# Two transformer stacks on one core: row sums with the squares stationary, a reciprocal of 128x4, and three output tiles side by side

## The chip, the cores and the metric

The kernel runs on one core of a Trainium2 chip. The metric is the device time of one execution in microseconds, taken as the median of several runs. Three runs of the kernel before gave 3040.9, 3040.95 and 3041.47 us.

## The reference

Two small stacks of two layers each run one after the other over a sequence of 512 tokens and a width of 1024. The first has sparse, windowed and dilated attention, the second a forgetting attention with a short convolution, a recurrent unit (RG-LRU), cross attention to a memory of 256 tokens, and gated feed-forward blocks. What the change touches are norms:

```python
def rmsnorm(x, g):
    x32 = x.astype(jnp.float32)
    y = x32 * lax.rsqrt(jnp.mean(x32 * x32, axis=-1, keepdims=True) + EPS)
    return y.astype(x.dtype) * g
...
    for layer in range(DEPTH):
        h = rmsnorm(x, g_mix_pre[layer])
        ...
        x = x + rmsnorm(y, g_mix_post[layer])
        h = rmsnorm(x, g_cross_pre[layer])
        m = rmsnorm(mem, g_mem[layer])
        y = memory_cross_attention(h, m, w_xq[layer], w_xkv[layer], w_xo[layer])
        x = x + rmsnorm(y, g_cross_post[layer])
        h = rmsnorm(x, g_ffn_pre[layer])
        y = swiglu(h, w_ffn_gu[layer], w_ffn_down[layer])
        x = x + rmsnorm(y, g_ffn_post[layer])
```

The first stack ends with such a norm over `x` too (`final`). So there are five places where the output of a linear, or `x` itself, is normed as a whole before anything can go on: `final` (after `dn1`), and the norms behind `xo0`, `dn2`, `xo1` and `dn3`. Four of them are followed at once by a norm ahead of a linear: `ab_in` (after `final`), `gu2` (after `xo0`), `c_u` (after `dn2`), `gu3` (after `xo1`). After the norm behind `dn3` comes the output.

## The kernel before

Activations lie feature-major: `x` is 128 partitions by 8 tiles (KT) by 512 tokens. A linear is a loop over output tiles of 128 features. Each sums 8 products (22 in the down projection) into one of the banks 0 to 3 of PSUM. The arithmetic is fp32 split in two parts, so a product is three matmuls of 128x512: `w_hi` by `xh`, `w_hi` by `xl`, `w_lo` by `xh` (lines 516 to 518).

The weights come as 462 chunks of 512 KB. They go through a ring of four slots (RING), and LEAD is 3. SyncE loads `w_raw`. ScalarE rounds it to `w_hi` (`high`, line 903, in its program order at the steps of each linear). GpSimd subtracts to get `w_lo` (`lows`, line 453). A slot is free again when TensorE is through the chunk (`chunk_done`), and an output bank when VectorE has evacuated it (`evac_done`).

A norm ahead of a linear is split. The gain goes into `xh` and `xl` before the product (`publish`), and the factor `rstd` of each token is multiplied in when the bank is evacuated (`scaled`, line 1276). `publish` for a tile m is, on ScalarE, the square into `acc` or `tmpa` (line 910) and then `xh` (line 915); on VectorE, the addition of the square to `acc` (line 1246) and then `xl` (line 1253). TensorE waits in the first output tile for each `xl` (`x_tile_ready`), and computes after that tile the sum over partitions with a matrix of ones (`sum_squares`, line 582), which leaves the sum of each token on all 128 partitions. `inverse_rms` is a scaling on VectorE (line 1264), the root on ScalarE (line 922), and the reciprocal on VectorE (line 1267), each over 128x512.

In the five places named above the same three steps stand with nothing beside them: TensorE has ended the linear, VectorE copies the last bank (line 1525, or adds it to `x`, line 1384), ScalarE squares it, VectorE adds, TensorE sums, then `inverse_rms`, and then per tile a multiplication by `rstd` (line 1529), an addition to `x` with a gain (line 1530), and `publish` of the tile before. At `final` the multiplication and the gain are one operation (line 1517).

Of the linears that follow, `gate_up` (`gu2`, `gu3`: 44 output tiles) works in pairs: tiles 2j and 2j+1 are evacuated, SiLU on ScalarE, product on VectorE, `hh` on ScalarE (line 1000), `hl` on VectorE (line 1363). ScalarE splits the weights of a pair at the head of the pair. `ab_in` has 25 tiles, of which tile 0 holds the logits of the forget gates. The sums of these (lines 1589 to 1600, a chain of small operations on 8x512) are computed on VectorE right after that tile. `c_u` has 8 tiles, each followed on VectorE by a convolution of four taps (lines 1652 and 1654) and a split (line 1660), and feeds the recurrent unit.

The order on each engine is the order of its program; engines meet at semaphores alone.

## Time and profile before

| | |
|---|---|
| median of 3 runs | 3040.95 us |
| the profiled execution | 3041.29 us, its span 3039.5 us |
| TensorE busy | 2818.8 us (93%), mean granted clock 0.961 |
| VectorE busy | 1111.0 us (37%) |
| ScalarE busy | 1089.0 us (36%) |
| GpSimd busy | 1314.0 us (43%) |
| DMA | 251.75 MB, mean 83 GB/s |

Times in the rows below are in microseconds from the start of the span unless ns is said. PE is TensorE, PEld its weight loads, DVE VectorE, ACT ScalarE, POOL GpSimd. L516 is line 516 of the kernel.

### The profile page before, as it was taken

What the parts mean: (1) busy time and instruction counts of PE and PEld (TensorE: products, weight loads), DVE (VectorE), ACT (ScalarE), POOL (GpSimd) and SP (SyncE); (2) the same over time, 40 slices, a digit from 0 to 9 for tenths busy, and PEclk for the clock granted to TensorE, in tenths of its full rate; (3) what the DMA queues carried; (4) which work ended last, traced back from release to release, by engine and by line L of the source; (5) the groups of instructions that cost most, each with busy time, mean ns of one, the idle gap of its engine ahead of it and who ended that gap; (6) DMA issues with size and microseconds to landing.
All of it is one profiled execution on the core that took longest, in us unless ns stands there. A gap on an engine that the chain in (4) does not pass through costs nothing.

```text
span 3039.5 us, 37582 instructions
## 1 busy us (share of the span) xinstructions
PE 2818.8 (93%) x13318; PEld 2219.7 (73%) x13318; DVE 1111.0 (37%) x1969; ACT 1089.0 (36%) x1761; POOL 1314.0 (43%) x691
## 2 busy tenths in 40 slices
PE   7999999999989999979998979999878789799997
PEld 5757788888657888857768857888756578588885
DVE  5674322113553222051547342221184472522202
ACT  5665322223663232232244333222225343323221
POOL 4555444444484444424446424444423364244442
PEclk9999999999999999999999989999989899799998
DMA  4301232333202223313113112233212231122331
GB/s 150 117 2 49 90 97 92 96 102 94 76 12 90 92 90 97 101 62 97 62 56 124 57 56 89 91 97 98 96 49 70 90 125 49 62 90 90 96 104 56
DMA packets 69088, 251.75 MB, mean 83 GB/s; under 512 B 7672, under 2 KB 7928, under 8 KB 68736
## 3 DMA queue, kind: packets, MB, share of 16 engines
q1 hardware_dynamic: 67104, 244.35, 25.5%
q10 hardware_dynamic: 1888, 6.14, 0.6%
q8 instruction: 59, 0.97, 0.1%
q14 instruction: 37, 0.30, 0.0%
HBM read 248.36 MB, written 2.10 MB: 82 GB/s over the span
## 4 chain that ended last, share of the span: by engine, by line
PE 83%; DVE 11%; issue 2%; ACT 2%; POOL 1%; DMA 0%; DVEq 0%; POOLq 0%; ACTq 0%
PE ps L516 25%; PE ps L517 25%; PE ps L518 25%; PE ps L611 3%; PE ps L636 2%; PE ps L622 2%; DVE acc L1246 1%; DVE xl L1253 1%; DVE rstd L1267 1%; DVE x L1530 1%; PE ps L582 1%; DVE y_mid L1529 1%; POOL pr L490 1%; DVE u_r L1654 1%; DVE u_r L1652 1%
## 5 line engine op out<-in xcount | busy, mean ns | idle before, releaser
L453 POOL TENSOR_TENSOR w_lo<-w_raw,w_hi 128x1024 fp32r<-128x1024 f32 x462 | 1117.2, 2420 | 1552.6 <-ACT w_hi L903 1547.6
L516 PE MATMUL ps<-xh,w_hi 128*128 128x512 f32 x2384 | 968.7, 406 | 88.3 <-DVE xl L1253 77.3
L517 PE MATMUL ps<-xl,w_hi 128*128 128x512 f32 x2384 | 959.2, 402 | 0.0
L518 PE MATMUL ps<-xh,w_lo 128*128 128x512 f32 x2384 | 944.6, 396 | 0.0
L903 ACT ACTIVATE w_hi<-w_raw 128x1024 fp32r<-128x1024 f32 x462 | 485.1, 1053 | 591.5 <-PE ps L518 590.7
L516 PEld LDWEIGHTS ps<-xh,w_hi 128*128 128x128 f32 x2384 | 451.7, 189 | 234.1 <-issue 72.3
L518 PEld LDWEIGHTS ps<-xh,w_lo 128*128 128x128 f32 x2384 | 453.9, 190 | 114.2
L517 PEld LDWEIGHTS ps<-xl,w_hi 128*128 128x128 f32 x2384 | 453.9, 190 | 103.5 <-issue 3.2
L516 PE MATMUL ps<-hh,w_hi 128*128 128x512 f32 x704 | 278.5, 396 | 0.0
L517 PE MATMUL ps<-hl,w_hi 128*128 128x512 f32 x704 | 278.4, 396 | 0.0
L518 PE MATMUL ps<-hh,w_lo 128*128 128x512 f32 x704 | 278.4, 395 | 0.0
L996 ACT ACTIVATE tmpa<-tmpa 128x512 f32<-128x512 f32 x88 | 55.6, 632 | 458.8 <-DVE tmpa L1276 458.8
L1276 DVE TENSOR_TENSOR tmpa<-ps,rstd 128x512 f32<-128x512 f32 x88 | 60.8, 691 | 415.2 <-PE ps L518 415.1
L490 POOL TENSOR_SCALAR pr<-pr,wgt 128x256 f32<-128x256 f32 (+3 forms) x160 | 158.1, 1001 | 94.7 <-DVE wgt L1340 94.4
L958 ACT ACTIVATE pr<-pr,negm 128x512 f32<-128x512 f32 (+2 forms) x224 | 120.1, 536 | 115.2 <-DVE negm L1326 115.1
L517 PEld LDWEIGHTS ps<-hl,w_hi 128*128 128x128 f32 x704 | 132.3, 188 | 31.9
L518 PEld LDWEIGHTS ps<-hh,w_lo 128*128 128x128 f32 x704 | 132.4, 188 | 31.9
L516 PEld LDWEIGHTS ps<-hh,w_hi 128*128 128x128 f32 x704 | 132.4, 188 | 31.9
L1276 DVE TENSOR_TENSOR tmpb<-ps,rstd 128x512 f32<-128x512 f32 x96 | 66.4, 692 | 180.6 <-PE ps L518 180.1
L1384 DVE TENSOR_TENSOR x<-ps,x 128x512 f32<-128x512 f32 x32 | 22.1, 692 | 286.2 <-PE ps L518 286.2
L1326 DVE CUSTOM_DVE_ANT_0 pr<-ps,tab 128x512 f32<-128x512 f32 (+2 forms) x192 | 85.5, 477 | 73.1 <-PE ps L611 72.0
L910 ACT ACTIVATE tmpa<-x 128x512 f32<-128x512 f32 x77 | 48.5, 630 | 165.9 <-DVE x L1384 101.0
(234 smaller groups left out, 2877.5 us busy)
## 6 DMA issues: line engine op xcount, KB each, us to landing
w_raw<-weights_in SPq DMA_DIRECT2D x462, 512.0 KB, 3.5
x<-x_in ACTq DMA_DIRECT2D x4, 512.0 KB, 10.3
mem<-mem_in ACTq DMA_DIRECT2D x2, 1024.0 KB, 4.8
x_out<-x SPq DMA_DIRECT2D x4, 512.0 KB, 2.6
rope<-rope_in ACTq DMA_DIRECT2D x1, 512.0 KB, 11.9
tab<-tables_in ACTq DMA_DIRECT2D x2, 256.0 KB, 2.9
tab<-tables_in ACTq DMA_DIRECT2D x1, 384.0 KB, 12.3
small<-small_in ACTq DMA_DIRECT2D x1, 326.5 KB, 5.0
```

The lines of the kernel that those rows point to most:

```text
L453: nc.gpsimd.tensor_tensor(w_lo[:, slot], w_raw[:, slot], w_hi.bitcast(f32)[:, slot], ALU.subtract).then_inc(lo_ready, 1)
L490: ins = nc.gpsimd.tensor_scalar(p, p, w, None, ALU.mult)
L516: nc.tensor.matmul(dst, w_hi[:, slot, w], hi, start=first, stop=False)
L517: nc.tensor.matmul(dst, w_hi[:, slot, w], lo, start=False, stop=False)
L518: return nc.tensor.matmul(dst, w_lo[:, slot, w], hi, start=False, stop=last)
L611: last = nc.tensor.matmul(ps[:, S_BANKS[n % 3], 0:u["nk"]], q, k, start=c == 0, stop=c == parts - 1)
L622: last = nc.tensor.transpose(ps[:, PT_BANKS[a], tokens(kb)], pr[:, n % 8, tokens(kb)], ident[:])
L636: last = nc.tensor.matmul(ps[rows, g["bank"], tokens(column)], values[kb], pt[:, (n + a) % 4, tokens(kb)], start=st["opens"] and kb == 0, ...
L903: A(w_hi[:, s], w_raw[:, s], ACT.Copy).then_inc(hi_ready, 1)
L958: A(p, p, ACT.Exp, scale=-1.0, bias=negm[:, slot, a:a + 1], accum_out=den[:, slot, a:a + 1]).then_inc(p_ready, 1)
L1276: return V.tensor_tensor(dst, bank[0:rows, 0:n], r[0:rows, 0:n], ALU.mult)
L1326: V.tensor_tensor_reduce(out=pr[:, n % 8, 0:nk], in0=ps[:, S_BANKS[n % 3], 0:nk], in1=u["mask"], scale=-u["scale"], scalar=start, op0=ALU.add,
```

## The change

It does five things.

1. In the five exposed norms the square of the last tile is not added to `acc`. `row_sums` takes the squares as the stationary operand and one column of ones as the moving one: four matmuls for `acc` (tiles 0 to 6), four for the last square, which leave 128x4 sums (partition = token within its block of 128). Scaling, root and reciprocal run on this 128x4 tile `stat`. `broadcast_rows` turns it back: four matmuls with a column of `stat` broadcast to 128x128 as stationary and the identity as moving operand fill bank 7 (MISC) with the reciprocal roots on all partitions. The normed tiles are computed from that bank, into banks 4 to 6, and added to `x` from there. After `xo` and `dn` ScalarE squares the last tile straight from its bank, and VectorE copies it afterwards. The table of the root is loaded ahead (`load_root`).
2. In the norms ahead of `ab_in`, `gu2`, `c_u` and `gu3` the squares are added on GpSimd (`sum_up`), six additions of 128x512, and the last is again left to the matmuls. ScalarE makes `xh` before the square (`publish_first`).
3. The first three output tiles of these four linears run side by side: for each of the 8 input tiles the products of all three (`side_by_side_tiles`). Row sums and broadcast run inside tile 3, ahead of its second and fourth input tile. The bank is then copied to `rstd` (`inverse_rms_kept`).
4. ScalarE's `high` for step 0 of these linears moves: the chunk is split ahead of the publishing, and GpSimd's order follows.
5. In `ab_in` the forget sums move from tile 0 to tile 4 on VectorE, and ScalarE's part of them from steps 0 and 1 to steps 4 and 5.

The diff, cut to its core:

```diff
+TOGETHER = {"ab_in": 3, "gu2": 3, "c_u": 3, "gu3": 3}
...
+            def sum_up(name):
+                first = list(TOGETHER).index(name) * (KT - 1)
+                before = sum(ADDS[n] for n in SUMS[:SUMS.index(name)])
+                for m in range(1, KT - 1):
+                    pool.wait_ge(sq_ready, first + m + 1)
+                    if m > 1:
+                        pool.wait_ge(acc_ready, before + m - 1)
+                    nc.gpsimd.tensor_tensor(acc[:], acc[:], tmpa[:, m % 2], ALU.add).then_inc(acc_ready, 1)
...
+            lows(CHUNK0["out_o"] + LEAD, CHUNK0["ab_in"] + LEAD + 1)
+            sum_up("ab_in")
+            lows(CHUNK0["ab_in"] + LEAD + 1, CHUNK0["ab_out"] + LEAD)
...
+                        if k in hooks:
+                            hooks[k]()
...
+                def side_by_side_tiles(n_m):
+                    pe.wait_ge(evac_done, g0 + n_m - 4)
+                    pe.wait_ge(lo_ready, c0 + n_m)
+                    for k in range(n_k):
+                        ready(k)
+                        for m in range(n_m):
+                            hi, lo = rhs(m, k)
+                            last = product(ps[:, (g0 + m) % 4, 0:n], (c0 + m) % RING, k, hi, lo,
+                                           k == 0, k == n_k - 1)
+                            if k == n_k - 1:
+                                last.then_inc(chunk_done, 1)
...
+                together = TOGETHER.get(name, 1)
+                if together > 1:
+                    side_by_side_tiles(together)
+                    for m in range(together, RING):
+                        out_tile(m, None, {1: row_sums, 3: broadcast_rows} if m == together else {})
+                    first = 1
...
+            def row_sums():
+                accs.n += KT - 2
+                rows_s.next()
+                pe.wait_ge(vt_copied, vts.n)
+                pe.wait_ge(acc_ready, accs.n)
+                for t in range(TB):
+                    nc.tensor.matmul(ps[:, MISC, t:t + 1], acc[:, tokens(t)], ones[:, 0:1], start=t == 0,
+                                     stop=False)
+                pe.wait_ge(last_sq, rows_s.n)
+                for t in range(TB):
+                    last = nc.tensor.matmul(ps[:, MISC, t:t + 1], tmpa[:, 1, tokens(t)], ones[:, 0:1],
+                                            start=False, stop=t == TB - 1)
+                last.then_inc(ss_done, 1)
+            def broadcast_rows():
+                pe.wait_ge(rows_ready, rows_s.n)
+                for t in range(TB):
+                    last = nc.tensor.matmul(ps[:, MISC, tokens(t)], stat[:, 2, t:t + 1].broadcast_to([P, P]),
+                                            ident[:], start=True, stop=True)
+                last.then_inc(rstd_ready, 1)
...
+            def square_row(src, m):
+                if m >= 3:
+                    act.wait_ge(acc_ready, n_.acc.n + m - 2)
+                if m == KT - 1:
+                    n_.acc.n += KT - 2
+                    A(tmpa[:, 1], src, ACT.Square).then_inc(last_sq, 1)
+                    return None
+                return A(acc[:] if m == 0 else tmpa[:, m % 2], src, ACT.Square)
...
+            def publish_first(m, gname):
+                A(xh[:, m], x[:, m], ACT.Copy, scale=gain(gname, m)).then_inc(xh_ready, 1)
+                ins = square_row(x[:, m], m)
+                if ins is not None:
+                    ins.then_inc(sq_ready, 1)
...
+                    if i is None and j == 0 and name in TOGETHER:
+                        root_rows()
+                    else:
+                        high(c0 + 2 * j + LEAD, i, 4)
                     high(c0 + 2 * j + 1 + LEAD, i, 4)
...
+            def squares_out(name, y, n_k=1):
+                for m in range(KT):
+                    for q in range(n_k):
+                        high(CHUNK0[name] + n_k * m + q + LEAD)
+                    if m == KT - 2:
+                        load_root()
+                    if m < KT - 1:
+                        act.wait_ge(evac_done, BANK0[name] + m + 1)
+                        square_row(y[:, m], m).then_inc(xh_ready, 1)
+                    else:
+                        act.wait_ge(chunk_done, CHUNK0[name] + n_k * KT)
+                        square_row(ps[:, (BANK0[name] + m) % 4, :], m)
+                root_rows()
...
+            def renormed_first(name, gname):
+                high(CHUNK0[name] + LEAD)
+                for m in range(KT):
+                    act.wait_ge(x_ready, n_.x.next())
+                    publish_first(m, gname)
...
+            def inverse_rms_rows(eps):
+                dve.wait_ge(ss_done, n_.ss.next())
+                V.tensor_scalar(stat[:, 1], ps[:, MISC, 0:TB], 1.0 / D, eps, ALU.mult, ALU.add).then_inc(var_done, 1)
+                dve.wait_ge(sd_done, n_.sd.next())
+                V.reciprocal(stat[:, 2], stat[:, 1]).then_inc(rows_ready, 1)
+                dve.wait_ge(rstd_ready, n_.rows.next())
+            def inverse_rms_kept(eps):
+                inverse_rms_rows(eps)
+                link(V.tensor_copy(rstd[:], ps[:, MISC, :]))
...
-            inverse_rms(rstd, 1e-5)
+            inverse_rms_rows(1e-5)
             for m in range(KT):
                 x_updated(V.scalar_tensor_tensor(out=x[:, m], in0=x[:, m], scalar=gain("final", m),
-                                                 in1=rstd[:], op0=ALU.mult, op1=ALU.mult))
+                                                 in1=ps[:, MISC, :], op0=ALU.mult, op1=ALU.mult))
                 if m:
-                    publish(m - 1, "mix_pre0")
-            publish(KT - 1, "mix_pre0")
+                    publish_first(m - 1, "mix_pre0")
+            publish_first(KT - 1, "mix_pre0")
...
+            def copies_out(name, y, n_k=1):
+                for m in range(KT):
+                    if m < KT - 1:
+                        dve.wait_ge(chunk_done, CHUNK0[name] + n_k * (m + 1))
+                    else:
+                        dve.wait_ge(last_sq, n_.rows.n + 1)
+                    V.tensor_copy(y[:, m], ps[:, (BANK0[name] + m) % 4, :]).then_inc(evac_done, 1)
+                    if m < KT - 1:
+                        publish_square(m)
+            def add_normed_rows(y, name, gname=None):
+                x0 = n_.x.n
+                def normed(m):
+                    if m >= 3:
+                        dve.wait_ge(x_ready, x0 + m - 2)
+                    return mark(V.tensor_tensor(ps[:, 4 + m % 3, :], y[:, m], ps[:, MISC, :], ALU.mult))
+                def add(m, n):
+                    dve.wait_ge(dve_self, n)
+                    x_updated(V.scalar_tensor_tensor(out=x[:, m], in0=ps[:, 4 + m % 3, :], scalar=gain(name, m),
+                                                     in1=x[:, m], op0=ALU.mult, op1=ALU.add))
+                add(0, normed(0))
+                n = normed(1)
+                for m in range(1, KT):
+                    after = normed(m + 1) if m < KT - 1 else None
+                    add(m, n)
+                    n = after
+                    if gname:
+                        publish_first(m - 1, gname)
+                if gname:
+                    publish_first(KT - 1, gname)
...
+                if m == 4:
+                    forget_sums()
+                if m == 5:
```

## Rows read from the trace of the kernel before

**Rows 1.** The page, part 4: shares of the chain that ended last.
```profile
PE 83%; DVE 11%; issue 2%; ACT 2%; POOL 1%; DMA 0%; DVEq 0%; POOLq 0%; ACTq 0%
```

**Rows 2.** Waits of TensorE: us in total, times, longest.
```profile
PE ps L516 <- DVE xl L1253: 77.3, 33, 18.4
...
PE ps L516 <- DVEq L1598: 5.5, 1, 5.5
```

**Rows 3.** Stretches around norms; each engine's busy us and instructions, clock, DMA.
```profile
core 0: us, PE busy (x) PEld busy (x) DVE busy (x) ACT busy (x) POOL busy (x), PEclk, DMA share, GB/s
1322.03:1334.10 12.07, 2.04 (x2) 0.53 (x3) 8.34 (x9) 4.72 (x7) 0.00 (x0) 0.58 0.13 43
1334.10:1347.70 13.60, 8.83 (x24) 4.71 (x25) 12.77 (x20) 8.61 (x14) 1.06 (x1) 0.87 0.00 1
1347.70:1359.60 11.90, 11.90 (x51) 9.23 (x50) 9.17 (x7) 3.50 (x4) 3.70 (x2) 1.00 0.16 45
1371.15:1376.00 4.85, 4.85 (x13) 3.85 (x14) 2.65 (x4) 3.50 (x4) 3.06 (x2) 0.58 0.03 8
...
1807.36:1826.37 19.01, 12.91 (x25) 7.19 (x26) 17.04 (x26) 8.98 (x14) 1.99 (x1) 0.50 0.00 0
...
3017.07:3039.50 22.43, 1.10 (x2) 0.30 (x2) 16.94 (x21) 2.54 (x3) 0.00 (x0) 0.58 0.23 94
```

**Rows 4.** The chain in order of time around `xo0`: start, us, what.
```profile
1795.20 0.24 PE ps L518
...
1796.19 0.64 ACT tmpa L910
...
1797.70 1.30 PE ps L582 x2
...
1800.41 3.37 DVE rstd L1267
...
1803.80 0.70 DVE y_mid L1529
...
1804.52 0.75 DVE x L1530
...
1828.07 0.43 PE ps L516
```

**Rows 5.** The same chain, small matmuls of the first attention.
```profile
145.41 1.10 PE ps L726 x8
```

**Rows 6.** Groups by line and form: count, busy us and mean ns, idle.
```profile
L1340 DVE RECIPROCAL wgt<-den 128x2 f32<-128x2 f32 x112 | 17.4, 155 | 0.5 <-ACT pr L958 0.4
...
L982 ACT ACTIVATE lp<-lp 128x8 f32<-128x8 f32 x1 | 0.2, 209 | 0.0
```

**Rows 7.** Timeline while GpSimd subtracts, stage `xkv0`.
```profile
1616.16 5.14 POOL L453 TENSOR_TENSOR w_lo<-w_raw,w_hi 128x1024 fp32r<-128x1024 f32 x2 [7.89 <-ACT w_hi L903]
...
1616.43 2.63 DVE L1529 TENSOR_TENSOR y_mid<-y_mid,rstd 128x512 f32<-128x512 f32 x1
```

**Rows 8.** Instructions of line 1253, of tile `rstd`: ns min/median/max.
```profile
L1253 DVE SCALAR_TENSOR_TENSOR xl<-x,small,xh x80: 739/745/2884, 15.6 to 2647.8; 128x512 fp32r<-128x512 f32 x80
...
L1276 DVE TENSOR_TENSOR tmpb<-ps,rstd x96: 691/692/693, 318.2 to 2888.3; 128x512 f32<-128x512 f32 x96
```

**Rows 9.** The page, part 5: the costliest groups, the two that split weights.
```profile
L453 POOL TENSOR_TENSOR w_lo<-w_raw,w_hi 128x1024 fp32r<-128x1024 f32 x462 | 1117.2, 2420 | 1552.6 <-ACT w_hi L903 1547.6
...
L903 ACT ACTIVATE w_hi<-w_raw 128x1024 fp32r<-128x1024 f32 x462 | 485.1, 1053 | 591.5 <-PE ps L518 590.7
```

**Rows 10.** Timeline of VectorE, first and last of the forget sums.
```profile
1354.39 0.47 DVE L1590 TENSOR_SCALAR fw<-fw,small 8x512 f32<-8x512 f32 x1
...
1371.04 0.07 DVE L1600 MEMSET gated<- 128x8 f32 x1
```

**Rows 11.** The chain at `dn2` and at the first evacuation of `c_u`.
```profile
2193.51 0.25 PE ps L518
...
2230.65 0.70 DVE z_u L1276
```

157 lines of the change are left out of this document (93 added, 64 removed).

## The prediction

> **What bounds the kernel now.** First the chain that ended last [rows 1]: 83% of it is TensorE, 11% VectorE. So the kernel is a stream of matmuls with holes, and the question is what fills the holes. Second the waits of TensorE [rows 2]: the largest is 77.3 us in 33 waits for `xl` of line 1253, the low half of a normed input; one wait of 5.5 us is for VectorE's line 1598, the forget sums. Third the stretches around the norms [rows 3]. A product (one matmul of 512 columns) costs 11.90 us / 51 = 0.233 us at full clock, so an output tile of 24 products takes 5.6 us. Between the last product before a norm and the first after it lie 12.07 us at `final` (1322.03 to 1334.10). Then the first tile of `ab_in` runs at the pace of the publishing: 24 products in 13.60 us, and at `gu2` 24 products in 19.01 us with VectorE busy 17.04 of them and a granted clock of 0.50, that is 1.2 GHz. Fourth the chain through one norm, `xo0` [rows 4]: TensorE ends at 1795.44 (call it t), copy, square 0.64, sum, ones matmul 1.30, variance, root, reciprocal 3.37, and only at t+8.36 the first multiplication by `rstd`.
>
> **The change, part by part.** All offsets are from t, the end of the last product before the norm.
>
> 1. *The exposed chain, five times (`final`, `xo0`, `dn2`, `xo1`, `dn3`).* Removed: the last addition, the 128x512 ones matmul, and three 128x512 operations, the reciprocal of 3.37 us [rows 4] among them. Added: 16 matmul instructions with the squares stationary (4 token blocks, two parts, two instructions each), of which 8 run under ScalarE's square; three operations on 128x4; 8 instructions that turn the reciprocal back. For the matmul instructions the nearest row is 8 of 128x64 in 1.10 us [rows 5]; the trace has none with one moving column. Bounds: 0.5 us (hardly more than a start) and 2.1 us (the same at half clock) for 8; I take 1.0. For the 128x4 operations the nearest rows are 155 ns (128x2 reciprocal) and 209 ns (128x8 on ScalarE) [rows 6]; with hand-overs of 0.03 to 0.14 us I take 0.8 us for all three, bounds 0.6 and 1.3. The sum for `xo` and `dn`: square from the bank to t+0.7; first sums to t+1.0, second to t+2.1; 0.1; small operations to t+3.0; turning back to t+4.15; first multiplication at t+4.2 instead of t+8.4. The table load of the root is now ahead; it lay under the sums before, so I count it at nothing.
> The Trainium skill (TensorE: Matmul & The Clock Gate, section LDWEIGHTS) gives a weight load as its columns over 1.2 in ns, whatever the rows, and says that fast loading does not hold for fp32: 107 ns for 128 columns, an estimate of 0.85 us for 8 where the row has 1.10. By it each group would be 0.2 us cheaper.
>
> 2. *The publishing.* VectorE now gives one tile per multiplication (0.70), addition (0.75) and `xl` (0.745) [rows 4, 8]: 2.2 us instead of 2.65 (its 17.04 us over the tile less the sum of 0.68). The order in the new helper puts two multiplications and two additions ahead of the first `xl`, and ScalarE now makes `xh` before the square: `xl` 0 is ready at t+8.4 (4.2 + 0.7 + 0.75 + 0.65 + 0.65 + 0.75 + 0.7) instead of t+11.9. At `final` there is one multiplication per tile, but a residual of 0.7 stands ahead of the square: first multiplication at t+4.7, `xl` 0 at t+7.4 (t+12.07 before).
>
> 3. *The sums on GpSimd.* A 128x1024 subtraction takes 2420 ns [rows 9], so 128x512 about 1.2 us, an estimate; bounds 0.8 and 1.6. What it does to VectorE is the disputed cost. A multiplication of two SBUF operands that began 0.27 us after a GpSimd operation took 2.63 us instead of 0.70, until about where that ended [rows 7]; `xl`, also two SBUF operands, goes from 739 to 2884 ns, while 96 multiplications that read a bank and SBUF lie between 691 and 693 ns [rows 8]. In the new code the multiplication goes from SBUF and the broadcast bank into a bank, the addition reads that bank and `x`: only `xl` is exposed. GpSimd's addition m starts 1.4 us after `x` m (xh 0.71, square 0.63) and ends at 2.6, while `xl` m comes one period P later at the earliest, and waits 2.6 - P where P is shorter: P = 2.2 + (2.6 - P), so P = 2.4 us per tile. At `final`, P = 1.5 + (2.6 - P) gives 2.05.
> The Trainium skill (SBUF — State Buffer, section "Who interferes with whom") has it as an exclusive lock: a VectorE instruction with two SBUF inputs contends with a GpSimd instruction that reads SBUF, one with at most one SBUF input outside the two-port modes does not, and the second to issue blocks until the first ends. The rows agree, 2.63 against 692 ns; whether a bank as destination changes that, no row shows.
>
> 4. *Three tiles side by side.* TensorE has 9 products per published tile, 2.1 us, where it had 3. The block starts after several us of idling, so at half clock: [rows 3], the stretch from 1371.15, has 13 matmul records in 4.85 us at 0.58, about 4 us at half pace before it rose. The first k costs 3.9 us, the rest 2.4 by VectorE (2.1 at `final` by TensorE). Block end at t+8.4+7x2.4+2.1 = t+27.4 (`final`: 7.4+3.9+7x2.1 = t+26.0). Tile 3 then holds the row sums (16 instructions, 2.05 us) and the broadcast (1.02): 8.7 us. Before, tile 3 of `gu2` began at 1828.07 [rows 4] plus two tiles and 0.6 of half clock, 1839.9 = t+44.5. The gain is 44.5 - 27.4 - 3.1 = 13.9 us, and the same at `gu3`, the one other norm of this kind ahead of a `gate_up`: 27.8.
> The ring of four weight chunks is drained by the block: chunk c0+4 is split by ScalarE (1.05 [rows 9]) only behind the root, ready about 6 us after the block, against 8.7 for tile 3; chunk c0+5 waits in `gate_up` for the SiLU and the copy of pair 0, ready at 13.1 against 14.3. So 1.2 us of slack is left. If that cover goes, each us late costs one, once per linear.
>
> 5. *`ab_in`.* The forget sums, 16.7 us of VectorE (1354.39 to 1371.11 [rows 10]), move from tile 0 to tile 4. Tile 4 ends at t+26.0+8.7+5.6 = t+40.3. While VectorE is in them TensorE has banks for tiles 5 to 7 (16.9 us), and tile 8 waits until 17.5: 0.6 us. Tile 8 begins at t+57.8 = 1379.8. Before: tile 4 at 1371.15, 4.2 us for 10 products, 86 more at 0.233: 1395.5. Gain 15.7.
>
> 6. *`c_u`.* Here VectorE's convolution is the bound after the norm (8 tiles between 2230.65 and the end of the stage), so what counts is when the first evacuation can begin: before at 2230.65, t+36.9 with t = 2193.76 [rows 11]. After: block end 27.4, k0 0.7, row sums 2.05, k1 and k2 1.4, broadcast 1.15, copy to SBUF 0.7: t+33.4. Gain 3.5. The convolutions themselves do not change.
>
> 7. *The end.* After `dn3` (t = 3017.07) nothing hides VectorE: 22.43 us [rows 3] lose 4.0 of the chain and up to 0.7 by the staggered order: 4.3.
>
> Sum: 27.8 + 15.7 + 3.5 + 4.3 = 51.3 us. The profiled execution took 3041.3 us (span 3039.5), the median is 3040.95, so the base is one and the same: 3041.3 - 51.3 = 2990.
>
> **The rivals.**
> A. *GpSimd's additions hold up every VectorE operation of the block*, bank or not. For it: the 2.63 us and the 2884 ns of [rows 7, 8]; against: the 691 to 693 ns of [rows 8]. Period 3.4 us (2.7 at `final`): block ends 6.9 us later at three places and 2.4 at `final`, 51.3 - 23 = 28 us gained, 3013.
> B. *The clock stays at 1.2 GHz through the block*, as it did through the tile from 1807.36 [rows 3]. Nine products then cost 3.87 us a k, the block ends at t+39.4, 12 us later at four places: gain 3, 3038. Against it: there TensorE was busy 12.91 of 19.01 us at half pace with holes; now it is without holes, and from 1371.15 the clock rose in about 4 us.
> C. *The drained ring turns into a lasting wait* (slower side). In `gate_up` the split of a chunk stands behind SiLU and copy of the pair before. If the block leaves ScalarE and GpSimd late by more than the slack and they don't catch up, each of the 82 remaining tiles of `gu2` and `gu3` waits; from 51/82 = 0.63 us a tile the change loses, at 0.8 us it is 3041.3 - 51.3 + 66 = 3056. Against it: both are idle more than half of the time (1552.6 us idle on GpSimd before the splits [rows 9]), so a delay should be worked off.
> D. *The change helps only at the front*: the small matmuls at their upper bounds, slow bank writes of VectorE (1.0 instead of 0.7), additions of 1.6 us on GpSimd. Each chain +1.5 (5 times, 7.5), each block +3 (4 times, `c_u` included): 32 gained, 3009.
>
> **How the numbers follow.** Forecast 0.69, A 0.09, B 0.03, C 0.05, D 0.10; 0.04 for an unforeseen clock gain or a faster block, down to 2980. The range 2979 to 3007 holds the forecast, the better side and part of D. Faster (by over 0.2%, 6 us, what a measurement of this kernel can tell from no change) 0.92, same 0.03, slower 0.05.
>
> **What would show it.** Reciprocals of 3353 ns fall from 17 of 128x512 to 8; first `xl` about 8.4 us after the last product at `xo0`, 7.4 at `final`; `xl` pitch 2.4 and 2.05 us; tile 3 of `gu2` begins at t+27 and lasts 8 to 9 us; the multiplication into a bank at 0.7 us. The forecast is wrong if the VectorE multiplications of the block stretch beyond 1 us (A), if the clock in it is 0.5 throughout (B), or if waits for `w_lo` appear in `gate_up` (C).

## The result and the profile after

The changed kernel takes 2928.77 us (median of four executions, 2925.7 to 2932.0) against 3041.21; the ratio is 0.963, 95% interval [0.9616, 0.9639]. The gain of 112 us is more than twice the 51 forecast and lies outside the range. The profiled execution, 2932.0 us with a span of 2930.2, is the slowest of its four.

The page of the kernel after, busy time of the engines and shares of the chain that ended last [rows 1]:

```profile
PE 2762.4 (94%) x13516; PEld 2252.8 (77%) x13516; DVE 1078.1 (37%) x1941; ACT 1085.9 (37%) x1766; POOL 1345.6 (46%) x715
...
PE 86%; DVE 9%; issue 2%; ACT 2%; POOL 1%; DMA 0%; DVEq 0%; POOLq 0%; ACTq 0%
```

TensorE got 198 instructions more and is busy 56 us less. Shorter norms take waits away; by themselves they don't take 56 us off the time for which the engine works. The waits of TensorE in the kernel after [rows 2] show the part that was forecast: 77.3 us for `xl` have become 21.6 + 15.0 (two lines), and the wait for the forget sums is gone.

```profile
PE ps L548 <- POOL w_lo L467: 27.6, 10, 5.1
PE ps L548 <- DVE xl L1380: 21.6, 4, 18.6
...
PE ps L548 <- DVE xl L1390: 15.0, 4, 4.2
```

Stretches of the kernel after [rows 3]: the gap at `final` and the block behind it, then the gap at `xo0` and the block of `gu2`, then the end; columns as in rows 3.

```profile
1290.24:1298.15 7.91, 4.07 (x26) 3.64 (x24) 3.34 (x7) 3.44 (x6) 2.35 (x1) 0.68 0.25 77
1298.15:1318.00 19.85, 19.85 (x79) 16.28 (x79) 11.37 (x13) 8.07 (x14) 9.31 (x6) 0.87 0.06 24
...
1751.39:1760.24 8.85, 3.97 (x25) 3.62 (x24) 5.13 (x10) 3.76 (x7) 2.34 (x1) 0.64 0.37 119
1760.24:1780.00 19.76, 19.76 (x84) 16.32 (x84) 13.89 (x18) 7.95 (x13) 7.75 (x6) 0.90 0.00 1
2912.16:2930.20 18.04, 3.97 (x25) 3.59 (x23) 11.27 (x19) 0.80 (x2) 0.00 (x0) 0.56 0.29 116
```

The gap is 7.91 us where it was 12.07, the tail 18.04 where it was 22.43, and in the blocks TensorE has no hole.

**Where the rest came from.** `gu0` is reached before any edited step: 352 times three matmuls with no wait, in both kernels. It took 248.43 us before and 240.27 after. One stretch within it, in the kernel before and then in the kernel after, TensorE alone (us, busy and matmul records, clock, DMA share, GB/s):

```profile
400.00:500.00 100.00, 100.00 (x428) 1.00 0.31 94
```

```profile
400.00:500.00 100.00, 100.00 (x443) 1.00 0.31 100
```

At the same granted clock and with no idle time 443 matmuls fit where 428 did: 0.226 us each against 0.234. The change adds a tile `stat` of 48 bytes a partition, and everything allocated behind it, `xh`, `hh` and `hl` among it, moves by 64 bytes, while `w_hi`, `w_lo` and `xl` stay. The distance from `w_hi` to `xh` was 72640 bytes, 64 short of a multiple of 256; now it is 72704, a multiple.

The account, stage by stage (end of a stage's last product to the end of the next one's), by the spans of three profiled executions: before, before with 48 unused bytes at that place (`pad48_before`, below), after.

| | us |
|---|---|
| span before | 3039.4 |
| placement alone, all stages | -64.1 |
| `gu2` -12.75, `gu3` -14.85, `ab_in` -15.21, `c_u` -5.16, end -4.56 | -52.5 |
| forget attention (stage to the end of `ab_out`) | +9.5 |
| rest (the first stack's attentions) | -2.2 |
| span after | 2930.1 |

### The profile page after: what moved, and what is told of

Same layout as the page of the kernel before. It is cut to its first block, busy times and chain, and to the rows that moved or that the text cites. A ratio compares the mean times of both kernels' runs of the same rounds, so it can differ in the third digit from the quotient of the medians.

```text
span 2930.2 us, 37914 instructions
## 1 busy us (share of the span) xinstructions
PE 2762.4 (94%) x13516; PEld 2252.8 (77%) x13516; DVE 1078.1 (37%) x1941; ACT 1085.9 (37%) x1766; POOL 1345.6 (46%) x715
## 4 chain that ended last, share of the span: by engine, by line
PE 86%; DVE 9%; issue 2%; ACT 2%; POOL 1%; DMA 0%; DVEq 0%; POOLq 0%; ACTq 0%
PE ps L548 26%; PE ps L550 25%; PE ps L549 25%; PE ps L686 4%; PE ps L711 2%; PE ps L697 2%; DVE acc L1373 1%; DVE xl L1380 1%; POOL pr L514 1%; DVE u_r L1839 1%; DVE u_r L1837 1%; DVE tmpb L1862 0%; DVE pr L1473 0%; DVE y_mid L1683 0%; PE ps L656 0%
## 5 line engine op out<-in xcount | busy, mean ns | idle before, releaser
L548 PE MATMUL ps<-xh,w_hi 128*128 128x512 f32 x2384 | 940.0, 394 | 50.4 <-DVE xl L1380 21.6
L549 PE MATMUL ps<-xl,w_hi 128*128 128x512 f32 x2384 | 933.3, 391 | 0.0
L550 PE MATMUL ps<-xh,w_lo 128*128 128x512 f32 x2384 | 933.0, 391 | 0.0
L548 PEld LDWEIGHTS ps<-xh,w_hi 128*128 128x128 f32 x2384 | 451.5, 189 | 150.3 <-issue 52.5
L548 PEld LDWEIGHTS ps<-hh,w_hi 128*128 128x128 f32 x704 | 132.2, 188 | 27.4
L549 PEld LDWEIGHTS ps<-hl,w_hi 128*128 128x128 f32 x704 | 132.2, 188 | 27.4
L548 PE MATMUL ps<-mem_h,w_hi 128*128 128x256 f32 x256 | 79.3, 310 | 20.4 <-POOL w_lo L467 20.4
```

The source lines that it names most:

```text
L548: nc.tensor.matmul(dst, w_hi[:, slot, w], hi, start=first, stop=False)
L549: nc.tensor.matmul(dst, w_hi[:, slot, w], lo, start=False, stop=False)
L550: return nc.tensor.matmul(dst, w_lo[:, slot, w], hi, start=False, stop=last)
```

## The experiments

**Placement.** Four kernels differ from before or after by one unused tile.

```diff
# pad48_before (before + 48 B)          # pad128_before (before + 128 B)
+        pad = sb("pad", [P, 12])       +        pad = sb("pad", [P, 32])
# pad64_all (before, ahead of x and all weights)   # pad64_after (after, behind stat)
+        pad = sb("pad", [P, 16])                  +        pad = sb("pad", [P, 16])
```

`pad48_before`. 

> The kernel before with one unused tile of 48 bytes per partition in the place where the change puts its tile stat, so that xh, hh, hl and everything behind them lie 64 bytes further on, as after the change; no instruction differs. Both traces share no change in gu0, yet its 352 products take 240.27 us after and 248.43 before. Theory P (placement): the products go faster through the new addresses, gu0 takes 240.3, dn0 119.7, and the whole about 71 us less, 2970. Rival I (the instructions themselves, or their place in memory, make the pace): nothing changes, gu0 248.4, the whole 3041. Rival C (the chip or the execution was another): the pace of both kernels of this call is the same.

Measured 2973.92 us against 3042.56 for the kernel before beside it, ratio 0.977 [0.9755, 0.9788]: 68.6 us from 48 bytes that nothing uses. The same stretch of this kernel:

```profile
400.00:500.00 100.00, 100.00 (x443) 1.00 0.30 94
```

`pad128_before`. 

> The kernel before with an unused tile of 128 bytes per partition there: xh, hh and hl keep their remainder of 64 by 128. If the remainder by 128 decides (P128), the pace stays slow, gu0 248.4 and the whole 3041. If any other address was enough, or the remainder by 256, gu0 goes to 240.3 and the whole to 2970.

3027.12 us, ratio 0.9949 [0.9929, 0.9969]. The distance is now 64 over a multiple of 256: `gu0` takes 247.22, `dn0` 120.87 us (before 123.2, after 119.68). So 64 above isn't 64 below, the remainder by 128 isn't the whole rule, and neither branch of the expectation came. Nor does the distance alone settle it at 64: `dn1` has the same operands at the same addresses as `dn0` and kept 123.2 us. The stretches lie within `dn0` and within `dn1` of this kernel (80 us, busy and matmul records, clock, DMA share, GB/s):

```profile
580.00:660.00 80.00, 80.00 (x351) 1.00 0.34 105
1210.00:1290.00 80.00, 80.00 (x345) 1.00 0.34 105
```

`pad64_all`. 

> The kernel before with an unused tile of 64 bytes per partition ahead of everything: xh, hh, hl come to a remainder of 0 by 128, while x, the weight tiles and xl go from 0 to 64. If the moving operand alone counts, dn0 (both moving operands moved) is fast, 119.7. If the weights' place counts as much, or the distance between weights and moving operand, dn0 stays at 123.2 and the whole at 3041.

3042.13 us, ratio 1.0004 [0.9994, 1.0015], every stage as before (`gu0` 248.43). All addresses moved by 64 bytes and no distance: the distance counts.

`pad64_after`. 

> The changed kernel with an unused tile of 64 bytes per partition behind stat: xh, hh, hl are back at a remainder of 64 by 128. Theory P128: gu0 248.4, dn0 123.2, the whole 2929 + 71 = 3000, which is the change proper at the old placement and near my forecast of 2990. Rival I: 2929, gu0 240.3.

2974.18 us, ratio 0.9783 [0.9747, 0.982], executions from 2968.1 to 2990.8; neither 3000 nor 2929. `dn1` is at 123.2 us here too. With the placement of `pad128_before` the change is worth 53 us (3027.1 to 2974.2), near the 51 forecast; with the placement of the kernel after it is worth 45 (2973.9 to 2928.8). Both include the loss in the forget attention (below).

**The pace by itself.** TensorE alone; 28 groups of 48 matmuls, one source line each. This program leaves the whole model out and hands its input on, and it was executed once.

```diff
+    for k in range(48):   # one group for each d
+        matmul(ps[:, b, :], w[:, stationary k], mv[:, 512 + d // 4 + (k % 8) * 512 :][:, 0:512])
```

`pace_by_distance`. 

> TensorE alone, and the model is left out (the output is the input passed through): after 64 warm-up matmuls, 28 groups of 48 fp32r matmuls of 128x512 each, every stationary 512 B after the last and every moving operand 2048 B after the last, as in the model's products; between the groups only the distance from the stationary's row to the moving row differs, taken modulo 512 B: 0, then -256 to 256 in steps of 32, then 8, 16, -16, -8, 4, and repeats at 512, 1024, 64, -64 and 0. Theory (the pace of a product is set by this distance): the groups at 0, 512 and 1024 run at the pitch of 226 to 227 ns that the products of the changed kernel show, those at +64 at 229 to 232 ns and those at -64 at 233 to 238 ns, as in the kernels shifted by 128 B and before the change. Rival (the pace came from something else in the kernel that stat's size touches, VectorE's or ACT's banks for instance): all groups show one pitch within 1 ns.

Groups at distances 0, -224, -192, -64, +64, +256, 0 again and -16, in this order (the length of a window is 48 matmuls):

```profile
27.01:37.89 10.88, 10.88 (x49) 9.01 (x48) 0.00 (x0) 0.00 (x0) 1.00 0.01 2
48.77:59.98 11.21, 11.21 (x50) 9.00 (x49) 0.00 (x0) 0.00 (x0) 1.00 0.00 1
59.98:70.97 10.99, 10.99 (x49) 9.01 (x48) 0.00 (x0) 0.00 (x0) 1.00 0.00 0
104.62:115.82 11.20, 11.20 (x50) 9.03 (x49) 0.00 (x0) 0.00 (x0) 1.00 0.00 0
138.21:149.21 11.00, 11.00 (x50) 9.01 (x48) 0.00 (x0) 0.00 (x0) 1.00 0.01 1
205.24:216.12 10.88, 10.88 (x49) 9.01 (x48) 0.00 (x0) 0.00 (x0) 1.00 0.01 2
216.12:227.00 10.88, 10.88 (x49) 9.01 (x48) 0.00 (x0) 0.00 (x0) 1.00 0.00 0
249.33:260.66 11.33, 11.33 (x50) 9.12 (x49) 0.00 (x0) 0.00 (x0) 1.00 0.00 0
```

| distance, bytes | start to start, ns |
|---|---|
| 0, -256, 256, 512, 1024 | 226.7 to 227.6 |
| 64, -192 | 229.1, 229.1 (64 again 229.2) |
| 16 (one group) | 231.7 |
| all other multiples of 32, and 8 | 233.1 to 234.1 |
| -8, 4, -16 | 234.2, 235.3, 235.9 |

In this program, with one distance to a group, the theory holds: the pace goes with the distance, with a period of 256 bytes (each pair such as +64 and -192, or +192 and -64, agrees within 0.2 ns), and 0 is the best of those tried. `dn0` of the kernel before, where all three matmuls stood at -64, had 233.4 ns, and the group at -64 has 233.2; `dn0` of `pad128_before`, all at +64, had 228.9, and the groups at +64 have 229.1 and 229.2. Two things are not explained by this table: the three matmuls of `gu0` before (230.1, 235.4, 237.9 ns; only the second one's operand `xl` stood at 0), which together are slower than a group at either distance, and `dn1` at +64 with 233.3 ns.

**The norms without the block.**

```diff
-TOGETHER = {"ab_in": 3, "gu2": 3, "c_u": 3, "gu3": 3}
+TOGETHER = {}      # publish, sum_squares, inverse_rms, the order of high: as before in these four
```

`norms_only`. 

> The kernel after without tiles side by side: ab_in, gu2, c_u and gu3 publish and sum as before the change (128x512 sums on VectorE, the matmul with ones over the sums, 128x512 square root and reciprocal, rstd in SBUF), while the five norms that nothing hides keep squares stationary, the 128x4 reciprocal and the turn by matmuls, and the forget sums stay at tile 4. Placement as in the kernel after. Theory of the prediction: the gap of each of the five places stays short (7.9 to 8.9 us), gu2 and gu3 lose what three abreast gave, 9 to 10 us each, ab_in little of its 15.7 as the forget sums stay, c_u up to 2 us, so 20 to 25 us longer than the kernel after, ratio to before 0.970 to 0.972 (0.967 if the forget attention keeps the clock as before, which is worth 9.7 us). Rival (the gain of gu2 and gu3 came from the earlier operand alone): within 10 us of the kernel after.

2943.07 us, ratio 0.9673 [0.9657, 0.9689]. From the kernel after: `gu2` 261.15 us against 252.91, `gu3` 260.33 against 252.22, `ab_in` 155.12 against 150.66, `c_u` 64.67 against 65.73. The block together with all that goes with it (sums on GpSimd, `xh` first, 128x4 statistics inside tile 3) is worth 8.2, 8.1, 4.5 and -1.1 us; the forget attention takes 9 us less here and hides half of that. That is the ratio of 0.967 which the expectation gave for this case.

**Two abreast.**

```diff
-TOGETHER = {"ab_in": 3, "gu2": 3, "c_u": 3, "gu3": 3}
+TOGETHER = {"ab_in": 2, "gu2": 2, "c_u": 2, "gu3": 2}
```

`two_abreast`. 

> The kernel after, with two output tiles side by side instead of three at the four first projections. Theory of the prediction's period: the third tile is 24 products (some 5.4 us at 0.2268 us), and the block of three ended about where its last operand landed, t+27.4; with two tiles the block's operands still land at t+26 to t+27 and one tile more is left behind them, less what the block waited: 3 to 5.4 us longer at ab_in, gu2 and gu3 each, c_u up to 5: 10 to 20 us in all, a ratio to before of 0.966 to 0.969. Rival (the third tile only fills time that the ring or the clock gives back anyway): no difference within 0.2%.

2929.6 us, ratio 0.9635 [0.9619, 0.9651], no difference from after. By stages the third tile is worth 2.4 us at `gu2`, 4.0 at `gu3`, nothing at `ab_in`, and costs 2.2 at `c_u`; the forget attention was 4.6 us shorter in this execution. The sum hid the parts. The theory's price, 3 to 5.4 us, came only at `gu3`.

**Sums on VectorE.**

```diff
-                for m in range(1, KT - 1):        # GpSimd: sum_up
+                for m in range(1, 1):
+                if 0 < m < KT - 1:                # VectorE: behind xl of tile m
+                    dve.wait_ge(sq_ready, n_.sq + 1); accumulate(m)
```

`sums_on_vector`. 

> The kernel after, with the six sums of squares of each first projection (tiles 1 to 6) put on VectorE behind each low part instead of on GpSimd. Theory of the prediction (a low part costs VectorE 1.35 us beside a GpSimd add and 0.74 us alone, and the period is set by VectorE): the period becomes 0.69 (high part taken off the path) plus 0.74 plus the sum's 0.68 to 0.74 and its wait, 2.1 to 2.9 us against 2.2 to 2.4 now, so 0 to 4 us longer per place and 0 to 12 us in all. Rival (the lock costs more than the sum on VectorE would): the kernel gets faster, by up to 1.5 us at each of three places, 0.15%.

2929.7 us, ratio 0.9631 [0.9615, 0.9647]; `ab_in`, `gu2`, `c_u` and `gu3` each agree with after within 0.05 us. The timeline of VectorE and GpSimd shows why, first in the kernel after (start, us, engine, line), then in this one:

```profile
2547.31 0.74 DVE L1390 SCALAR_TENSOR_TENSOR xl<-x,small,xh 128x512 fp32r<-128x512 f32 x1
...
2548.75 1.28 POOL L501 TENSOR_TENSOR acc<-acc,tmpa 128x512 f32<-128x512 f32 x1 [2.78 <-ACT tmpa L1004]
...
2549.23 1.34 DVE L1390 SCALAR_TENSOR_TENSOR xl<-x,small,xh 128x512 fp32r<-128x512 f32 x1
...
2551.76 0.73 DVE L1390 SCALAR_TENSOR_TENSOR xl<-x,small,xh 128x512 fp32r<-128x512 f32 x1
```

```profile
2549.23 0.74 DVE L1391 SCALAR_TENSOR_TENSOR xl<-x,small,xh 128x512 fp32r<-128x512 f32 x1
...
2549.89 0.68 DVE L1374 TENSOR_TENSOR acc<-acc,tmpa 128x512 f32<-128x512 f32 x1
...
2551.76 0.74 DVE L1391 SCALAR_TENSOR_TENSOR xl<-x,small,xh 128x512 fp32r<-128x512 f32 x1
```

Beside GpSimd's addition `xl` takes 1.34 us instead of 0.74. The extra 0.6 us is about the addition of 0.68 that left VectorE. The period alternates between 1.92 and 2.53 us in the kernel after and is 2.52 in this one. TensorE needs 2.04 us for the 9 matmuls of an operand and has a backlog from its first microseconds at the lower clock, so that it has no hole in the block of either kernel: it sets the block's end, and the difference doesn't show.

**The forget sums first.**

```diff
-                if m == 4:
+                if m == 0:      # ahead of the evacuation on VectorE; ScalarE's part at steps 0 and 1
                     forget_sums()
```

`forget_sums_first`. 

> The kernel after, with the forget gate's sums put back ahead of tile 0 of ab_in instead of at tile 4, its bank evacuated at tile 1. Theory of the prediction: VectorE is held 15 to 16.5 us by the sums before the low parts are published, the products wait for them, and the time lengthens by 13 to 16 us (ratio to before about 0.968). Rival (the products hide most of it, as three tiles side by side need operands only every 5 us): 3 us or less.

2936.7 us, ratio 0.9657 [0.9641, 0.9673]. `ab_in` takes 158.36 us for its products in place of 142.75, 15.6 more, as the theory had it and about all that this stage had gained; but the forget attention behind it has its gap of 60.1 us back. The whole is only 7.9 us longer than after (2928.8): over half of what the move gains in `ab_in` is lost again in the next stage.

**The forget attention.** The gap from the last product of `ab_in` to the first of `ab_out` was 59.9 us before and in three padded kernels (59.9 to 60.1), and 69.7 after. The instructions up to 5.8 us into it start at the same offsets. There the two part; the scores of 128 columns, in the kernel before and then in the kernel after:

```profile
1497.04 0.49 PE L611 MATMUL ps<-k_f,q_f 64*128 64x128 f32 x4 [0.79 <-DVE negm L1326]
```

```profile
1446.74 0.80 PE L686 MATMUL ps<-k_f,q_f 64*128 64x128 f32 x4 [0.79 <-DVE negm L1473]
```

In the kernel after TensorE is slow 1.6 us sooner in the stage and stays so far longer, though in both the last 50 us ahead of it were products at full clock without a hole. The whole gap in the kernel before, in the kernel after and in `best` (below), columns as in rows 3:

```profile
1491.20:1551.10 59.90, 54.05 (x386) 35.19 (x384) 28.80 (x106) 31.04 (x92) 34.23 (x32) 0.91 0.04 10
1440.90:1510.60 69.70, 64.49 (x385) 41.63 (x383) 29.40 (x106) 31.26 (x92) 35.29 (x32) 0.76 0.03 8
1437.79:1526.40 88.61, 84.31 (x394) 54.75 (x392) 29.88 (x106) 31.88 (x92) 35.39 (x32) 0.58 0.02 7
```

The granted clock is a mean of time at 2.4 GHz (1.00) and at 1.2 GHz (0.50). It accounts for the gaps: the share not granted is 59.9 x 0.09 = 5.4 us, 69.7 x 0.24 = 16.7 us and 88.6 x 0.42 = 37.2 us, so 11.3 and 31.8 us more than before, where the gaps are 9.8 and 28.7 us longer. Gaps of kernels without throw-away matmuls in this stage, each read from one execution:

| kernels | gap, us | mean clock |
|---|---|---|
| before, `norms_only`, `forget_sums_first` | 59.9, 60.1, 60.1 | 0.91 |
| `two_abreast`, `warm_blocks`, `warm_blocks_c_u_2` | 65.2, 65.2, 65.3 | 0.82 |
| after, `sums_on_vector`, `pad64_after` | 69.7, 69.7, 69.8 | 0.76 |

`norms_only` and `forget_sums_first` have the tile `stat` and the placement of the kernel after and a gap of 60, and `pad64_after` has another placement and a gap of 69.8: it isn't the placement. `attention_later` puts throw-away matmuls ahead of the scores; two runs change their number, one applies them to the kernel before, one puts them inside the stage.

```diff
+            for k in range(8):      # 4 in attention_later_4, 16 in attention_later_16; before_later: 8
+                nc.tensor.matmul(ps[:, MISC, :], xh[:, k % 4, tokens(0)], xh[:, 4 + k % 4, :], start=True, stop=True)
             attention(UF, {})
# warm_attention instead, behind the scores of each step:
+                    if steps is UF and s < 4:
+                        for k in range(4):
+                            nc.tensor.matmul(ps[:, MISC, :], xh[:, k % 4, tokens(0)], xh[:, 4 + k % 4, :],
+                                             start=True, stop=True)
```

`attention_later`. 

> The kernel after with eight throw-away matmuls of 128x512 (1.8 us) ahead of the forget attention's scores, and nothing else. Theory (the moment at which the clock falls is a matter of phase: it fell 5.8 us into the stage in the kernels after and 7.4 us in those of before, with the same instructions up to there): shifted by 1.8 us the fall comes at another point of the stage and the gap is another one, 58 to 67 us in place of 69.7. Rival (the work itself, or what ran before it, decides): 69.7 plus 1.8, 71.5 us.

2922.26 us, ratio 0.9606 [0.9587, 0.9625], gap 61.8 us at a mean clock of 0.92. Less the 1.8 us of the throw-away matmuls that is 60.0, the gap of the kernel before.

`attention_later_4`. 

> The kernel after with four throw-away matmuls (0.9 us) ahead of the forget attention's scores, half as many as in the run with eight, whose gap was 61.8 us against 69.7. Theory (the fall of the clock comes at a moment that the work before sets, and a later start of the attention puts more of it behind the fall or ahead of it): a gap of 60.7 or of 66 to 71 us, one of the values seen so far (59.9, 65.2, 69.7) plus 0.9. Rival (eight matmuls kept the clock up by their activity, and four do half of it): between these, about 66.

2930.29 us, ratio 0.9628 [0.9606, 0.965], gap 65.3 at 0.84, nearer to the rival's 66 than to the theory's values; its two executions are 8 us apart.

`attention_later_16`. 

> The kernel after with sixteen throw-away matmuls (3.6 us) ahead of the forget attention's scores. Theory of phase: one of the values seen so far plus 3.6, that is 63.5, 68.8 or 73.3 us. Rival (activity: the more, the better the clock holds): at most 63.5, with a shorter stretch at the lower clock than with eight.

2929.07 us, ratio 0.9624 [0.9605, 0.9643], gap 64.9 at 0.89. Neither the theory's values nor the rival's bound.

`before_later`. 

> The kernel before the change with eight throw-away matmuls (1.8 us) ahead of the forget attention's scores. Theory of phase: the kernel before stood at a good phase (gap 59.9), and shifted by 1.8 us it can fall into a bad one: the gap becomes 61.9 to 71.7 us. Rival (activity or the content of the stage): 61.7, nothing but the matmuls' own time.

3042.92 us, ratio 1.0004 [0.9992, 1.0017], gap 62.1: in the profiled execution the shift alone, no bad phase. Of the eight executions one, without a profile, took 3054.5 us at a mean clock of 0.957, the others 3041.3 to 3043.5 at 0.960 to 0.962.

`warm_attention`. 

> The kernel after with four throw-away matmuls of 128x512 in each of the first four steps of the forget attention, behind its scores, in a bank that is free then. In the kernel after the scores of 128 columns take 0.80 us from 5.8 us into this stage, in the kernel before the change 0.49 us there, and the lower clock lasts until 37 us in, against 20 us; the stage's gap is 69.7 us against 59.9. Theory (the fall of the clock is answered to by what PE does in its first microseconds): the clock holds or falls later, and the gap becomes 57 to 62 us, less 8 to 12 us, plus the 0.9 us a step that the throw-away matmuls cost. Rival (the fall comes anyway): the gap grows to 71 to 74 us.

2922.34 us, ratio 0.9605 [0.9589, 0.9621], gap 62.7 at 0.92, within what the theory had. (By the granted clock the lower level ends 40 us into the stage in the kernel after and 17 in the kernel before; the 37 and 20 of the expectation are rough.) The stage's 20 us from 16 us behind `ab_in`'s end, in the kernel after, in `attention_later` and in `best` (below):

```profile
1456.90:1476.90 20.00, 20.00 (x86) 12.29 (x85) 7.45 (x27) 7.53 (x22) 9.07 (x8) 0.50 0.00 0
```

```profile
1456.06:1476.06 20.00, 19.50 (x144) 12.34 (x143) 10.73 (x40) 12.05 (x37) 13.64 (x13) 0.98 0.00 1
```

```profile
1455.80:1475.80 20.00, 20.00 (x85) 12.54 (x85) 7.13 (x27) 7.82 (x23) 9.12 (x8) 0.50 0.00 1
1475.80:1495.80 20.00, 20.00 (x90) 12.80 (x88) 6.32 (x22) 6.75 (x21) 9.12 (x8) 0.50 0.00 1
```

86 matmuls at 0.50 against 144 at 0.98 in the same time: a busy share of 100% says nothing here, the clock column does.

**Awake at the blocks, and the best version.**

```diff
                     pe.wait_ge(lo_ready, c0 + n_m)
+                    for k in range(14):
+                        nc.tensor.matmul(ps[:, g0 % 4, :], w_hi[:, c0 % RING, tokens(k % 4)],
+                                         w_hi[:, c0 % RING, T:2 * T], start=True, stop=True)
# best: range(10) at ab_in only, c_u 2 abreast, 8 matmuls as in attention_later
# warm_both: range(14), c_u 2 abreast, and warm_attention; warm_blocks_c_u_2: the same without the last
```

`warm_blocks`. 

> The kernel after with 14 throw-away matmuls of 128x512 in the wait before each block of three tiles (their bank is overwritten by the first product). Theory: in the kernel after the block's first products run at the lower clock (0.43 us from one matmul to the next for 3 to 4 us), PE gets a backlog of some 9 matmuls x 0.2 us = 2 us, and the block's end is set by PE and not by VectorE's period; kept awake it starts at full clock and the block ends where the last low part lands plus 9 matmuls: 0.5 to 2 us earlier at each of four places, 2 to 8 us in all, plus what the clock does further on. Rival (the granted clock doesn't answer to such matmuls, or VectorE sets the end anyway): no difference, within 0.2%.

2918.98 us, ratio 0.9593 [0.9577, 0.9609], 10 us less than after by medians and 7 by the profiled executions. By stages the blocks give 1.3 us at `ab_in`, 0.7 at `gu2`, 0.1 at `c_u` and nothing at `gu3`; 4.5 came from the forget attention. Only at `ab_in` do the throw-away matmuls run past the first `xl`, by 2.1 us. At `c_u` and `gu3` that `xl` itself comes 0.6 and 0.9 us later than in the kernel after. In the blocks of `gu2`, `c_u` and `gu3` TensorE now waits up to 0.2 us for an `xl`, so little more is to be had there; the theory's upper end was wrong.

`best`. 

> The kernel after with what the runs so far point to: c_u with two tiles side by side in place of three (2.2 us), ten throw-away matmuls in the wait ahead of ab_in's block (1.3 us), eight ahead of the forget attention's scores (8.0 us if the phase is right again, 0 to 8 if not). 2916 to 2920 us against 2929, a ratio to before of 0.959. Rival (ab_in's earlier end shifts the fall of the clock again): no better than 2922.

2928.99 us, ratio 0.9618 [0.9601, 0.9635], executions from 2923.8 to 2944.2; the profiled one, 2944.15 us, had a gap of 88.6 us in the forget attention (rows above), with the same eight matmuls ahead of the scores as `attention_later`. The rival was right, and more.

`warm_both`. 

> The kernel after with fourteen throw-away matmuls ahead of each block of tiles side by side, four in each of the first four steps of the forget attention, and two tiles side by side at c_u. The run with the last alone had a gap of 62.7 us in that stage, with the same throw-away matmuls at the blocks one of 65.2 without them. Theory (the matmuls within the attention hold the clock whatever the phase; the run with eight of them ahead of the stage and an earlier end of ab_in fell to 88.6 us): the gap stays at 61 to 64 us, and the time is 2912 to 2917 us (2919 less 2.2 at c_u and 1 to 3 in the stage), with executions closer together than the 20 us seen there. Rival (phase decides here too): a gap of 65 to 75 us in some execution, a spread of more than 8 us.

2918.85 us, ratio 0.96 [0.9582, 0.9617], executions from 2916.0 to 2923.2, gap 61.0 at 0.94. The spread is the theory's; the median is 2 us above its range.

`warm_blocks_c_u_2`. 

> The same without the matmuls inside the forget attention: the run of warm blocks (2919 us) with two tiles side by side at c_u in place of three. Theory: 2.2 us less, 2917 us. Rival (c_u with two abreast only looked shorter because its clock recovered sooner, and the throw-away matmuls already give that): 2919.

2924.26 us, ratio 0.9617 [0.9592, 0.9641], executions from 2921.6 to 2932.7. That is 5 us more than `warm_both`, with a gap of 65.3 us against 61.0, which points to the matmuls inside the stage; but the two intervals overlap, and `warm_blocks` without them was at 2919 too. `c_u` took 55.69 us for its products, the theory's 2 us less, lost among the rest.

So `warm_blocks` and `warm_both`, at 2919 us, are faster than both kernels: their slowest executions (2924.8 and 2923.2) are below the fastest of the kernel after (2925.7).

## Why the prediction was wrong

**The step that failed** is the last line of the sum: "so the base is one and the same: 3041.3 - 51.3". It takes the product's 0.233 us [rows 3] for a constant, in the stages that the change doesn't touch too. Nothing in the diff adds or removes a product; but its tile `stat` moved the moving operands by 64 bytes against the weights, and the product went to 0.227 us. Over some 10,700 matmuls of this kind that is about the 64 us (profiled spans) to 69 us (medians) that `pad48_before` shows by itself. The row was right for its kernel and no price of a step. A tile declared ahead of others is an edit to everything behind it, and I gave it none.

**A second term was missing**, with the other sign: +9.5 us in the forget attention. The prediction ended part 5 at tile 8 of `ab_in` and asked nothing of the stage behind. The profiled execution is 3.2 us above its median, so the median may hold less of it. By medians the 112 us are 68.6 of placement and 45 of the change with this loss in it.

**The change's own steps stood.** At equal placement:

| | forecast | measured |
|---|---|---|
| first multiplication, `xo0` / `final` | t+4.2 / 4.7 | t+4.7 / 5.5 |
| first `xl` ready, `xo0` / `final` | t+8.4 / 7.4 | t+8.7 / 7.8 |
| period of `xl`, `gu2` / `ab_in` | 2.4 / 2.05 | 1.9 and 2.5 in turn / 1.7 |
| end of the block, `gu2` / `ab_in` | t+27.4 / 26.0 | t+27.1 / 26.8 |
| tile 3 | 8.7 | 8.2 |
| tile 8 of `ab_in` | t+57.8 | t+58.1 |
| gain `gu2`, `gu3` | 13.9, 13.9 | 12.8, 14.9 |
| gain `ab_in` | 15.7 | 15.2 |
| first evacuation of `c_u` | t+33.4 | t+32.0 |
| gain `c_u` | 3.5 | 5.2 |
| gain at the end | 4.3 | 4.6 |
| sum | 51.3 | 52.5 |

Some of these agree partly by luck. Tile 3 at 0.233 us a product would have lasted 8.4. The end of the block at `gu2` was worked out from VectorE's period, 7 times 2.4 us and the last 9 products; the trace has it otherwise. The last `xl` is ready at t+22.7, and TensorE, 3.9 us in the first 9 matmuls at half clock and 2.04 in each later nine, is busy from the first to the last and ends at t+27.1. The period of `xl` had no part in that. And the errors of single gains, from -1.1 to +1.7 us, leave only 1.2 in the sum. The small operations of part 1, in the kernel after at `xo0` (t = 1751.39):

```profile
1751.38 0.95 PE L644 MATMUL ps<-ones,acc 128*128 128x1 f32 x8
...
1752.23 1.05 PE L648 MATMUL ps<-ones,tmpa 128*128 128x1 f32 x8
1753.32 0.16 DVE L1407 TENSOR_SCALAR stat<-ps 128x4 f32<-128x4 f32 x1 [0.42 <-PE ps L648]
1753.52 0.20 ACT L1019 ACTIVATE stat<-stat 128x4 f32<-128x4 f32 x1 [1.34 <-DVE stat L1407]
...
1753.76 0.18 DVE L1409 RECIPROCAL stat<-stat 128x4 f32<-128x4 f32 x1 [0.27 <-ACT stat L1019]
...
1753.99 2.07 PE L656 MATMUL ps<-ident,stat 128*128 128x128 f32 x8 [0.70 <-DVE stat L1409]
...
1756.10 0.70 DVE L1704 TENSOR_TENSOR ps<-y_mid,ps 128x512 f32<-128x512 f32 x1 [2.17 <-PE ps L656]
```

Eight matmul instructions with one moving column take 0.95 and 1.05 us, where the prediction took 1.0. The three operations on 128x4 took 0.67 us with their hand-overs, 0.8 forecast. The turn back was put at 1.15 and took 2.07: TensorE was at half clock by then, as the stretches of the sums and of the turn show.

```profile
1751.39:1753.30 1.91, 1.90 (x17) 1.81 (x15) 0.69 (x1) 0.60 (x1) 0.00 (x0) 1.00 0.63 165
1753.99:1756.06 2.07, 2.07 (x8) 1.78 (x8) 0.00 (x0) 0.68 (x1) 1.31 (x1) 0.50 0.01 4
```

At `dn2` it took 1.16, the first multiplication came at t+3.8 and the gap was 7.94 us instead of 8.85. So the chain is half a microsecond late where the turn finds TensorE at half clock (`xo0`, `dn3`), and 0.4 early where it doesn't (`dn2`, `xo1`). The estimate of 0.85 us for eight from the Trainium skill (TensorE: Matmul & The Clock Gate, section LDWEIGHTS) was too low by 0.1 to 0.2 us, at a granted clock of 1.00.

**The rivals.** A (GpSimd holds up all of VectorE) fell: all 32 multiplications into a bank took 680 to 697 ns, and six of them ran beside an addition on GpSimd for 0.5 us. Only `xl` was held, for 0.6 us in every second period or so (0.4 at `ab_in`, 1.0 once), as the rule of the lock in the Trainium skill (SBUF — State Buffer, section "Who interferes with whom") has it for two SBUF inputs; with a bank among its operands the multiplication was free of it. B (the clock stays down) fell: in the block of `gu2` the clock is 0.90 over 19.8 us, and at `gu3` only the first 9 or so matmuls are 0.43 us apart, the others 0.23. C (the drained ring in `gate_up`) fell: `gu2` and `gu3` have no wait for `w_lo` at all, in either kernel. In all these waits were 22.0 us in 7 before and are 27.6 in 10; what is new stands in `c_u`, where the prediction had no such term. The waits of TensorE there (2131 to 2190 us):

```profile
PE ps L548 <- POOL w_lo L467: 7.1, 3, 5.1
```

Three tiles abreast have 7.1 us of it there, two have 3.2 and the kernel without the block has 0.5, while `c_u` takes 65.7, 63.5 and 64.7 us. So the drained ring probably is what the third tile costs in `c_u`; no run takes this wait out by itself. The reciprocals of 128x512 fell from 17 to 8.

**What stays open.** What sets the moment and the length of the fall in the forget attention. The gap was 59.9 to 88.6 us with the same instructions from the scores on, and the granted clock accounts for it; what decides the clock isn't shown. With 4, 8 and 16 matmuls ahead the gap less their own time is 64.4, 60.0 and 61.3 us, against 69.7 with none. That by itself would fit plain activity nearly as well as the moment. Against activity stands `best`, with the same eight matmuls ahead and 88.6 us. A rule of the moment isn't found either: by the granted clock the fall comes some 8.2 us into the gap in `best` and 8.8 in `attention_later`, and they differ by 27 us. All of it rests on one profiled execution a kernel, while executions of one kernel spread over 20 us. And why the pace depends on the distance between the operands was only measured, not explained, with `dn1` at +64 as an exception.

## What to carry to other kernels

Before a kernel bound by TensorE is priced step by step, check what its new tiles do to the addresses of matmul operands; look at a stage that the change doesn't touch first, as it tells placement from mechanism at once. Try the rows of weights and of moving operands a multiple of 256 bytes apart: in this kernel that was worth more than five reworked norms. Judge a moved piece of work by its stage and the next one together, and read a stage's clock column before its busy share.

## What the runs showed of the hardware

- fp32r matmuls of 128x512 at full clock follow each other every 226.7 to 227.6 ns where the distance from stationary to moving row is a multiple of 256 bytes, 229.1 at +64, 231.7 at +16 and 233 to 236 at the others tried (`pace_by_distance`). `dn1` of `pad128_before` had 233.3 at +64. All addresses 64 bytes further on made no difference (3042.1 against 3042.6 us, `pad64_all`).
- `xl` with both tensors that it reads in SBUF took 1.34 us beside a GpSimd addition of 1.28 us, 0.74 alone; a multiplication from SBUF and a bank into a bank took 0.68 to 0.70 either way (kernel after).
- At equal instructions a stage that alternates between small matmuls (64 or 8 rows, transposes of 128x128) and VectorE took between 59.9 us (mean granted clock 0.91) and 88.6 us (0.58). Executions of one kernel then spread over 20 us (`best`, 2923.8 to 2944.2).
